# Index scores of the sparse attention: the sum over heads moved from VectorE to TensorE

## The reference, cut to what matters

```
qi = partial_rope(qi.reshape(B, S, IDX_HEADS, IDX_HEAD), pos)      # 16 heads of 64
ki = partial_rope(ki.reshape(B, S, 1, IDX_HEAD), pos)[:, :, 0]
wi = wi * (IDX_HEADS ** -0.5 * IDX_HEAD ** -0.5)                   # one weight for each query and head
...
rel = relu(einsum('bqhd,bsd->bqhs', qib, ki))
score = einsum('bqhs,bqh->bqs', rel, wib)
score = where(causal, score, -1e30)
_, idx = top_k(score, 64)
```

## Time and profile before

| what | value |
|---|---|
| median of 3 runs | 3442.95 us (3433.09 to 3447.68) |
| the profiled execution, own time | 3442.06 us |
| its span in the trace | 3440.3 us |
| mean granted PE clock | 0.879 of full speed |
| PE busy, of the span | 2518.5 us (73%) |
| DVE busy, of the span | 1717.8 us (50%) |

### The profile page before, as it was taken

The page is one execution under the profiler, slowest core; times in us unless marked ns, Lnnn a source line. Parts: engine busy times, 40 slices in busy tenths (PEclk is TensorE's granted clock), DMA queues, the critical chain, the costliest instruction groups (busy, mean ns, idle before and its releaser), DMA issues.

```text
span 3440.3 us, 42202 instructions
## 1 busy us (share of the span) xinstructions
PE 2518.5 (73%) x15833; PEld 1976.6 (57%) x15833; DVE 1717.8 (50%) x2295; ACT 1082.5 (31%) x2108; POOL 2598.3 (76%) x1837
## 2 busy tenths in 40 slices
PE   7989886989999999989999899107602840472077
PEld 5866785779988998889988679103201310230032
DVE  4053467143300132230412436897797879788954
ACT  6434423464444444454545554001000000000000
POOL 7887824868999999988866578886687578657852
PEclk9999998999999999999999999658856875796589
DMA  5665400546655666556544355899999999999998
GB/s 180 220 176 159 128 3 3 175 129 173 185 192 188 181 183 189 187 150 172 153 130 129 105 171 170 363 427 427 427 428 427 427 427 427 427 426 427 427 427 344
DMA packets 241028, 868.10 MB, mean 252 GB/s; under 512 B 18830, under 2 KB 21390, under 8 KB 174284
## 3 DMA queue, kind: packets, MB, share of 16 engines
q0 software_dynamic: 73776, 536.97, 37.0%
q1 hardware_dynamic: 163414, 316.11, 30.2%
q10 hardware_dynamic: 3668, 12.75, 1.2%
HBM read 860.24 MB, written 2.10 MB: 251 GB/s over the span
## 4 chain that ended last, share of the span: by engine, by line
PE 49%; POOL 20%; DMA 11%; DVE 6%; issue 4%; ACT 1%; DVEq 0%; ACTq 0%; POOLq 0%
PE acc L1937 19%; PE acc L1947 19%; DMA zone<-in_peer_v,zone 11%; POOL zone L734 9%; POOL lasting L734 9%; PE acc L1943 3%; PE acc L2075 3%; PE acc L2501 2%; POOL w_lo L615 2%; DVE lasting L1878 1%; PE acc L2390 1%; DVE zone L1487 0%; PE acc L1984 0%; ACT w_hi L779 0%; DVE x_lo L1616 0%
## 5 line engine op out<-in xcount | busy, mean ns | idle before, releaser
L615 POOL TENSOR_TENSOR w_lo<-lasting,w_hi 128x512 fp32r<-128x512 f32 (+1 forms) x1184 | 1607.6, 1378 | 328.1 <-ACT w_hi L779 307.9
L779 ACT ACTIVATE w_hi<-lasting 128x512 fp32r<-128x512 f32 (+1 forms) x1184 | 741.5, 631 | 916.6 <-PE acc L1937 473.2
L2501 PE MATMUL acc<-zone,lasting 128*128 128x512 f32 x512 | 254.5, 655 | 700.2 <-ACT lasting L1285 639.9
L2501 PEld LDWEIGHTS acc<-zone,lasting 128*128 128x128 f32 x512 | 104.8, 210 | 849.2 <-ACT lasting L1285 500.5
L734 POOL DMA_INDIRECT zone<-in_peer_v,zone x128 | 193.4, 1511 | 173.5 <-DVE lasting L1878 75.4
L1947 PE MATMUL acc<-x_hi,w_hi 128*128 128x256 f32 (+1 forms) x1856 | 306.0, 287 | 14.8 <-POOL w_lo L615 5.8
L1848 DVE CUSTOM_DVE_ANT_0 zone<-lasting,zone 128x2048 f32<-128x2048 f32 x128 | 293.4, 2292 | 29.8 <-DMA lasting<-in_peer_u,zone 20.7
L1848 DVE CUSTOM_DVE_ANT_0 zone<-zone 128x2048 f32<-128x2048 f32 x128 | 293.4, 2292 | 23.0 <-DMA zone<-in_peer_u,zone 14.1
L1947 PE MATMUL acc<-x_lo,w_hi 128*128 128x256 f32 (+1 forms) x1856 | 299.0, 283 | 0.0
L1947 PE MATMUL acc<-x_hi,w_lo 128*128 128x256 f32 (+1 forms) x1856 | 298.8, 283 | 0.0
L734 POOL DMA_INDIRECT zone<-in_peer_u,zone x128 | 258.0, 2016 | 49.8 <-issue 37.5
(11 more groups left out here) (417 smaller groups left out, 3881.6 us busy)
## 6 DMA issues: line engine op xcount, KB each, us to landing
lasting<-in_w_in SPq DMA_DIRECT2D x200, 512.0 KB, 3.6
lasting<-in_w_up SPq DMA_DIRECT2D x128, 512.0 KB, 3.8
lasting<-in_w_down SPq DMA_DIRECT2D x128, 512.0 KB, 3.6
lasting<-in_w_mix_out SPq DMA_DIRECT2D x32, 512.0 KB, 3.6
lasting<-in_w_out SPq DMA_DIRECT2D x32, 512.0 KB, 3.6
lasting<-in_peer_w_query SPq DMA_DIRECT2D x32, 512.0 KB, 3.6
lasting<-in_w_kv_cross SPq DMA_DIRECT2D x16, 512.0 KB, 3.7
lasting<-in_w_q_cross SPq DMA_DIRECT2D x8, 512.0 KB, 3.6
```

The source lines that it names most:

```text
L615: pool.tensor_tensor(w_lo[:, k, 0:width], ring[:, slot, s % SLOT_SLABS, 0:width], w_hi[:, k, 0:width].bitcast(FP32), ALU.subtract).then_in ...
L779: act.activation(w_hi[:, s % PARTS, 0:width], ring[:, slot, s % SLOT_SLABS, 0:width], ACT.Copy).then_inc(hi_ready, 1)
L2501: last = pe.matmul(bank(4 * t + c), diag[:, n // 2, k], rows_buf[2 * n + k][:, c * CHUNK:(c + 1) * CHUNK], start=hx % 2 == 0 and i == 0 an ...
```

## The change

The weights of one head for 128 queries are put on the diagonal of a 128x128 matrix. Multiplying that matrix with the 128 x `nk` relu of the head gives the weighted relu, and with all 16 such products added in one accumulator bank (bank 5) TensorE makes the whole sum. DVE builds the 16 diagonals of a tile with one instruction on 128x2048 elements, two of them in all, before the first tile; afterwards it only adds the causal mask to bank 5.

```
+        head_diag = [at(Z + TILES * R_W, I_HEADS, P)]
...
+        head_diag.append(at(X0 + 8 * SEQ, I_HEADS, P))
...
 (VectorE)
                 sc = score[:, t, 0:nk]
-                step(dve.tensor_copy(sc, causal[:, t, META:META + nk]))
-                for i in range(I_HEADS // 2):
-                    m = t * (I_HEADS // 2) + i
-                    dve.wait_ge(s_rel, m + 1)
-                    for j in range(2):
-                        last = STT(sc, rel[:, m % 4, j, 0:nk], p[:, t, WI0 + 2 * i + j:WI0 + 2 * i + j + 1], sc,
-                                   ALU.mult, ALU.add)
-                        if j == 0:
-                            step(last)
-                    last.then_inc(s_acc2, 1)
-                    dve.wait_ge(s_acc2, m + 1)
+                if t == 0:
+                    for n in range(TILES):
+                        dve.wait_ge(s_rope, n + 1)
+                        TT(head_diag[n], ident.unsqueeze(1).to_broadcast([P, I_HEADS, P]),
+                           p[:, n, WI0:WI0 + I_HEADS].unsqueeze(2).to_broadcast([P, I_HEADS, P]), ALU.mult).then_inc(s_hdiag, 1)
+                dve.wait_ge(s_acc2, (t + 1) * I_HEADS // 2)
+                TT(sc, bank(5)[:, 0:nk], causal[:, t, META:META + nk], ALU.add).then_inc(s_sel, 1)
+                dve.wait_ge(s_sel, t + 1)
...
 (TensorE)
                 if t:
                     pe.wait_ge(s_qT2, t)
+                    pe.wait_ge(s_sel, t)
...
-                for i in range(I_HEADS // 2):
+                for i in range(I_HEADS // 2 + 2):
                     m = t * (I_HEADS // 2) + i
-                    if m >= 2:
+                    if i < I_HEADS // 2:
+                        if m >= 2:
+                            pe.wait_ge(s_rel, m - 1)
+                        for j in range(2):
+                            half = slice(j * I_HEAD, (j + 1) * I_HEAD)
+                            last = pe.matmul(bank(6 * (m % 2) + j)[:, 0:nk], qiT[half, t, i], kiT[half, 0:nk],
+                                             start=True, stop=True)
+                        last.then_inc(s_ix, 1)
+                    if i >= 2:
                         pe.wait_ge(s_rel, m - 1)
...
+                        if i == 2:
+                            pe.wait_ge(s_hdiag, t + 1)
+                        for j in range(2):
+                            last = pe.matmul(bank(5)[:, 0:nk], head_diag[t][:, 2 * (i - 2) + j], rel[:, (m - 2) % 4, j, 0:nk],
+                                             start=i == 2 and j == 0, stop=i == I_HEADS // 2 + 1 and j == 1)
+                        last.then_inc(s_acc2, 1)
...
-            pe.wait_ge(s_rel, I_HEADS)
+            pe.wait_ge(s_sel, TILES)
```

More of the change, by code:

```diff
@@ L276, in build @@
         kT = at(x_rest + R_W - 2 * SEQ, A_KV, SEQ)
+        head_diag.append(at(X0 + 8 * SEQ, I_HEADS, P))
+        assert X0 + 8 * SEQ + I_HEADS * P <= x_rest + R_W - 3 * SEQ
         y_sq = at(x_rest + 3 * R_W, R_W)
@@ L525, in build @@
         s_ang, s_trig, s_rope, s_kturn, s_kT2 = (sem(n) for n in ("angle_ready", "sines_ready", "rotated", "keys_turned", "keyT_ready"))
+        s_hdiag = sem("head_diagonals_ready")
         s_qturn, s_qT2, s_ix, s_rel, s_acc2, s_sel = (sem(n) for n in (
@@ L2213, in _ @@
                 nk = (t + 1) * P
-                for i in range(I_HEADS // 2):
+                for i in range(I_HEADS // 2 + 2):
                     m = t * (I_HEADS // 2) + i
-                    if m >= 2:
-                        pe.wait_ge(s_rel, m - 1)
[L2218 to L2222, removed]
+                    if i < I_HEADS // 2:
[7 more added lines that the diff above has]
+                    if i >= 2:
+                        pe.wait_ge(s_rel, m - 1)
+                        if i == 2:
[4 more added lines that the diff above has]
+                        last.then_inc(s_acc2, 1)
             def attend(m0, n, heads_n, scores_of, blocks, values, pr_of, pT_of):
```

## The result

The changed kernel took 3447.64 us (median of 12 runs, 3444.51 to 3453.31), the kernel before 3441.69 us (12 runs, 3433.09 to 3448.81): ratio 1.002, 95% interval 1.0011 to 1.0028. It is 6 us slower. The forecast was 3 us less.

What follows compares the result with a forecast made beforehand. Bound taken: the chain through VectorE's additions to tile 1's selection. Tile 0 wins 3.7 us, tile 1 gives back 0.7, so 3.0 us less: 3440.0 us median, chance 0.6, range 3431 to 3453.

Steps and rivals of the forecast that it cites:

- each pair costs TensorE 0.70 us in tile 0 and 1.30 us in tile 1: Index products plus weighted sums of two heads at full clock; TensorE sets the pace, six such turns per tile.
- The handshake rival: Weighted sums and relus wait for each other; 0.2 us at each of 16 pairs, 3.2 us, leaves no gain; chance 0.15.
- the choice of the full clock for the sums: All TensorE prices at 2.4 GHz; nearly pauseless full-row work from 545.5 to 550.8 was to keep granted clock at 1.00.
- The rival of the clock: Half clock from 547 on adds 3.6 us in tile 0, 12.3 us slower in all; chance 0.2 of losing over the gain.
- The stage is on the path to the end one for one: A microsecond won at the end of tile 1's additions, 569.76, should be a microsecond at the program's end.
- The loss of 3.0 us to GpSimd in tile 0: Second to fifth VectorE additions stretched by GpSimd's SBUF instructions: 4.48 us instead of 4 x 0.37.
- The diagonals were hidden: Two wide VectorE instructions from 539.6, 2.3 us each, second at most 3.5, fit in VectorE's wait before tile 0's sums.
- GpSimd's delay: The wide diagonal instructions hold up GpSimd's work that ended at 551.71, by 2.3 to 4.6 us.
- the square root was not late: ScalarE's square root, waiting for GpSimd, has a 5.5 us margin (561.8 - 556.3), so GpSimd's delay does not reach the end.
- The time after the reciprocal stayed the same: After the selection, order is kept: normalisation, stretched mask instruction (2.53 us) and attention move together with the reciprocal.
- the whole would stay within 0.5%: Measured time differs from before by no more than about 0.5%, 17 us; chance 0.92.

Runs made afterwards that it cites:

- filler run: Changed kernel plus 16 idle transposes on TensorE where it waits for ScalarE's two query copies, in both tiles: 3442.73 us, ratio to before 1.0004.
- full-row run: Changed kernel with index products on all 128 rows, keys stored twice with one half zero each: 3441.68 us, one run.
- stream with mask: Changed kernel reordered so TensorE never pauses between tiles, two pairs at a time, plus tile 1's mask through accumulator bank 4: 3431.33 us, ratio to before 0.9974.

## Why the prediction was wrong

*What failed first* is the term "each pair costs TensorE 0.70 us in tile 0 and 1.30 us in tile 1". The back-to-back prices in it were right (0.90 and 1.72 us for eight full-row instructions, 0.65 us for two pairs' products on half rows). But they come from rows of one shape. The changed kernel goes back and forth between half-row and full-row matmuls, and each change costs 0.18 to 0.20 us. Measured turns at full clock: 1.06 and 1.69. Over 6 and 6 such turns that is 6 x 0.36 + 6 x 0.39 = 4.5 us, which is what separates the filler run (32.1 us) from the forecast (27.6), and more than the 3.0 us of the forecast gain. The handshake rival had this size (3.2 us) but the wrong mechanism: with the same waits and one shape throughout nothing was left on top.

*What failed second* is the choice of the full clock for the sums. "Nearly without a pause, with full rows, which speaks for the full level" did not hold: in two of three executions of the changed kernel the clock fell behind the 2 us pause for ScalarE's copies and did not rise in 10.2 and 13.6 us that were mostly turns of products and sums. It rose only in the twelve sums in a row at the end of tile 0. That costs another 5 to 7 us when it happens. The rival of the clock had the mechanism and the place. It had too little for tile 0 (3.6 us; the selection came 5.8 us later than in the filler run, at 19.83 against 14.06: a turn took 1.88 us, not twice 0.70), and its 12.3 us in all were too many, because the level came back before tile 1. The Trainium skill (TensorE: Matmul & The Clock Gate, What's actually happening) says that sustained activity brings the full rate; the full-row run and the end of tile 0 agree with it, and the turns of tile 0 in these two executions do not.

*What held.* The stage is on the path to the end one for one: every difference of a stage found by profile lies within the interval of its medians (stream with mask 8.7 us by the stage, 9.3 in medians), though these intervals are some 6 us wide. The loss of 3.0 us to GpSimd in tile 0 is shown. The diagonals were hidden (2.28 us as worked out; the second 3.36 us, 3.5 allowed), GpSimd's delay was 3.8 us (2.3 to 4.6) and the square root was not late. The time after the reciprocal stayed the same (36.4 us before, 35.9 to 36.6 in the three profiles after). That the whole would stay within 0.5% held, and 3447.64 lies inside the range, which was wide because the runs of before were; the direction was wrong.

## What to carry to other kernels

The price of a matmul taken from a row holds for a run of equal ones; where matmuls on different rows of the array alternate, look for a row that alternates, or order them in groups. Work moved onto an engine whose clock depends on what it did before takes on that dependence: price it at both levels, and cover or remove the pause ahead of it. And look first at why the instructions that are to be moved take so long: here a third of the additions' time in tile 0 was another engine's, and one wait got it back; at the mask, one operand in the accumulator memory did.

## What the runs showed of the hardware

- A change between fp32 matmuls on 64 rows and on 128 rows costs 0.18 us at 128 columns and 0.20 us at 256, at full clock. The weight load at the change starts with its matmul and not 0.11 us ahead of it.
- The granted clock stayed at 0.50 for 13.6 us (548.2 to 561.9) in which TensorE had work all the time, most of it half-row products and full-row sums by turns. It rose in the last of twelve full-row instructions in a row, in this profile and in one more.
- The same kernel finds either clock level at the same place: stage times of 33.3, 38.2 and 39.4 us in three profiles.
- Two VectorE instructions went from 1.30 and 2.53 us beside GpSimd to 0.44 and 0.44 us when one operand of each (the output of the first, an input of the second) lay in the accumulator memory.
